# Experts in units of 32 tokens on four column quarters of the array, and weights in transfers of 4 KB rows

## The reference

```python
idx, wts = route(hf, w_router, b_router)       # best group of 4, then the top 2 of its 4 experts
# the rows of each expert are gathered, then
(silu(xe @ w_gate[e]) * (xe @ w_up[e])) @ w_down[e]   # D=1024 -> F=512 -> D=1024
# and each token adds its two rows, weighted by wts
```

## Time and profile before

| | us |
|---|---|
| median of 3 runs (2388.24 to 2390.66) | 2388.29 |
| profiled execution | 2393.53 |
| its span | 2391.9 |

### The profile page before, as it was taken

The page is one execution under the profiler, slowest core; times in us unless marked ns, Lnnn a source line. Parts: engine busy times, 40 slices in busy tenths (PEclk is TensorE's granted clock), DMA queues, the critical chain, the costliest instruction groups (busy, mean ns, idle before and its releaser), DMA issues.

```text
span 2391.9 us, 33087 instructions
## 1 busy us (share of the span) xinstructions
PE 2167.1 (91%) x12218; PEld 1202.3 (50%) x12219; DVE 1155.4 (48%) x2059; ACT 743.6 (31%) x1571; POOL 273.3 (11%) x465
## 2 busy tenths in 40 slices
PE   6999999999999399999998599989984899999991
PEld 2444444456666355555554367655443455555551
DVE  2355500678997622222222699999845122222225
ACT  3111100567775222222222411026252222222222
POOL 0000010000000112111112300000000111112113
PEclk8999999899999699999999699999986999999996
DMA  9166410003301665566666400300025777624646
GB/s 390 72 246 246 176 54 0 36 19 150 150 10 52 266 247 187 222 256 254 254 254 254 158 36 35 140 36 1 0 97 202 310 322 286 261 86 154 246 153 224
DMA packets 51578, 391.49 MB, mean 164 GB/s; under 512 B 9009, under 2 KB 9265, under 8 KB 33841
## 3 DMA queue, kind: packets, MB, share of 16 engines
q1 hardware_dynamic: 22514, 298.12, 30.9%
q0 software_dynamic: 28992, 92.40, 11.4%
HBM read 340.12 MB, written 50.37 MB: 163 GB/s over the span
## 4 chain that ended last, share of the span: by engine, by line
PE 77%; DVE 13%; DMA 5%; issue 2%; ACT 2%; POOL 0%; POOLq 0%; SPq 0%; DVEq 0%
PE ps L1417 21%; PE ps L1399 12%; PE ps L1265 9%; DVE kv L1134 8%; PE ps L1513 5%; PE ps L1283 5%; PE ps L1339 4%; PE ps L1297 3%; PE ps L1310 3%; PE ps L1322 3%; PE ps L1481 3%; DMA expert_rows<-hT 3%; PE ps L1406 2%; PE ps L1386 1%; DMA hT<-h_rows,idx_now 1%
## 5 line engine op out<-in xcount | busy, mean ns | idle before, releaser
L1134 DVE SCALAR_TENSOR_TENSOR kv<-kv,cols 128x640 f32<-128x640 f32 (+1 forms) x390 | 305.1, 782 | 13.3
L1417 PE MATMUL ps<-kv,hT 128*64 128x256 f32 x2624 | 290.9, 379 | 0.9 <-DMA kv<-in_w_gate_up 0.9
L1417 PE MATMUL ps<-ring,hT 128*64 128x256 f32 x2496 | 281.0, 384 | 10.8 <-issue 5.1
L644 ACT ACTIVATE hT<-ps 128x128 f32<-128x128 f32 x160 | 44.4, 277 | 679.8 <-PE ps L1417 679.8
L1417 PEld LDWEIGHTS ps<-kv,hT 128*64 128x64 f32 x2624 | 201.3, 137 | 101.4 <-issue 26.4
L1417 PEld LDWEIGHTS ps<-ring,hT 128*64 128x64 f32 x2496 | 193.2, 139 | 110.4 <-issue 39.7
L1453 PE MATMUL ps<-hT,ring 128*128 128x320 f32 (+1 forms) x768 | 225.4, 455 | 6.3 <-ACT hT L525 6.3
L1265 PE MATMUL ps<-hT,ring 128*128 128x512 f32 x512 | 226.5, 601 | 1.6 <-ACT hT L525 1.6
L904 DVE TENSOR_TENSOR_SCAN pbuf<-hT 128x128 f32<-128x128 f32 (+7 forms) x128 | 173.3, 1354 | 47.6 <-ACT hT L576 47.3
L1453 PEld LDWEIGHTS ps<-hT,ring 128*128 128x128 f32 x768 | 147.2, 193 | 81.1 <-ACT hT L525 7.0
L1069 DVE COPY hT<-ps 128x128 f32<-128x128 f32 x160 | 46.7, 292 | 267.3 <-PE ps L1406 267.3
(11 more groups left out here) (240 smaller groups left out, 2475.5 us busy)
## 6 DMA issues: line engine op xcount, KB each, us to landing
ring<-in_w_gate_up SPq DMA_DIRECT2D x32, 2048.0 KB, 12.5
kv<-in_w_gate_up SPq DMA_DIRECT2D x32, 2048.0 KB, 13.1
kv<-in_w_ada SPq DMA_DIRECT2D x20, 2048.0 KB, 7.6
ring<-in_w_down SPq DMA_DIRECT2D x16, 2048.0 KB, 13.9
kv<-in_w_down SPq DMA_DIRECT2D x16, 2048.0 KB
expert_rows<-hT POOLq DMA_DIRECT2D x160, 128.0 KB, 2.5
expert_rows<-ring POOLq DMA_DIRECT2D x2, 8192.0 KB, 24.7
ring<-in_w_in SPq DMA_DIRECT2D x8, 2048.0 KB, 8.1
```

What stands on the lines that cost most here:

```text
L1134: ins = V.scalar_tensor_tensor(new, old, w_dw_c[:, c, k:k + 1], new, ALU.mult, ALU.add)
L1417: ins = mm(bank(f)[UNIT * t:UNIT * t + UNIT, 0:2 * P], xT[:, c, :], wset[s][t][:, 512 * c + 256 * f:512 * c + 256 * f + 256], start=(c == ...
```

## The change

Units of 32 tokens; each expert gets at least `MINBLK = 2` blocks. A row is split over four partition quarters of 256 features, and matmuls have 32 stationary columns on one quarter of the array's columns. In gate/up a quarter makes gate and up of 128 hidden features, all four in one bank; down has 4 chunks x 4 quarters of 256 columns. One silu, one product and one transpose per block replace two of each.

Around it: down of block b-1 now stands behind gate/up of block b. Each expert's first block is written apart from the loop, since its down pass belongs to the expert before. Two gather buffers `xg[0]`, `xg[1]`; GpSimd copies a gathered block to `xs`, from which TensorE transposes. `yo_all` has two slots, and ScalarE stores them, in four transfers of 32 rows x 1 KB. Each weight piece goes in four transfers with rows of 4 KB. `TABLE` grows from 50 to 96. Semaphores of the weights are shared by the layers, and a small activation ahead of the final gathers (`rows_stored`) loads the table for the square root.

```diff
-UNIT = 64
-MAXBLK = (2 * T + E * (UNIT - 1)) // UNIT + 1
-TABLE = MAXBLK + 2
+UNIT = 32
+QUARTERS = P // UNIT
+MINBLK = 2
+MAXBLK = 2 * T // UNIT + MINBLK * (E - 2)
+TABLE = MAXBLK + 4
+PARTS = 4
+QUARTER = D // QUARTERS
...
+        xg = [hflat[:, QUARTER * u:QUARTER * (u + 1)] for u in range(2)]
+        xs = hflat[:, 768:768 + QUARTER]
+        xT = hflat[:, 512:768].rearrange("p (c t) -> p c t", c=DC)
+        sg, ha, haT = hflat[:, 1024:1152], hflat[:, 1152:1280], hflat[:, 1280:1408]
+        yo_all = hflat[:, 1792:1792 + 2 * QUARTER]
...
-                sp.dma_start(wset[s][k], src).then_inc(w_loaded[l][s][k], 16)
+                for q in range(PARTS):
+                    sp.dma_start(part(wset[s][k], q), part(src, q)).then_inc(w_loaded[s][k], 16)
...
-                        sp.wait_ge(up_done[l], 2 * ends)
+                        sp.wait_ge(up_done[l], ends)
...
+                            src = w_gate_up[ds(4 * i + 2 * s + 2 * l * E + k, 1)].rearrange("a p n -> (a p) n")
+                            for q in range(PARTS):
+                                sp.dma_start(part(wset[s][k], q), part(src, q)).then_inc(w_loaded[s][k], 16)
...
+                        src = w_down[ds(2 * i + s + l * E, 1)].rearrange("a p n -> (a p) n")
+                        for q in range(PARTS):
+                            sp.dma_start(part(wset[s][2], q), part(src, q)).then_inc(w_loaded[s][2], 16)
...
+                def gather(u):
...
+                        out=xg[u], out_offset=None, in_=h_dram[l].rearrange("t (q d) -> (t q) d", q=QUARTERS),
+                        in_offset=bass.IndirectOffsetOnAxis(ap=idx_now[:, u:u + 1], axis=0)).then_inc(x_gathered[l][u], 16)
...
+                pairs = pool.value_load(bounds[0:1, E + 1:E + 2], min_val=1, max_val=(MAXBLK + 1) // 2)
+                pool.wait_ge(x_gathered[l][0], 16)
+                nc.gpsimd.tensor_copy(xs, xg[0]).then_inc(idx_made[l], 1)
+                nc.gpsimd.tensor_copy(idx_now[:, 0:1], slot_tok[:, 2:3]).then_inc(idx_made[l], 1)
+                pool.wait_ge(idx_made[l], 5)
                 gather(0)
...
+                with pool.Fori(0, pairs) as i:
+                    for u in (1, 0):
+                        n = 2 * i + 2 - u
+                        pool.wait_ge(x_gathered[l][u], 16 * i + 32 - 16 * u)
+                        pool.wait_ge(x_turned2[l], n)
+                        nc.gpsimd.tensor_copy(idx_now[:, u:u + 1], slot_tok[:, ds(n + 2, 1)])
+                        nc.gpsimd.tensor_copy(xs, xg[u]).then_inc(x_ready[l], 1)
+                        pool.wait_ge(table_made[l], 1)
+                        pool.wait_ge(x_ready[l], n)
+                        gather(u)
+                pool.wait_ge(rows_stored[l], 1)
...
+                def silu(b):
+                    act.wait_ge(up_done[l], b + 1)
+                    nc.scalar.activation(sg, bank(0)[:, 0:P], ACT.Silu).then_inc(silu_done[l], 1)
+                def store(b, half):
+                    act.wait_ge(y_kept[l], b + 2)
+                    for q in range(QUARTERS):
+                        act.dma_start(y_dram[l][ds(b * UNIT, UNIT), QUARTER * q:QUARTER * (q + 1)],
+                                      yo_all[UNIT * q:UNIT * (q + 1), ds(half * QUARTER, QUARTER)]
+                                      ).then_inc(y_stored[l], 16)
...
+                blocks = act.value_load(bounds[0:1, E:E + 1], min_val=MINBLK * E, max_val=MAXBLK)
+                silu(0)
+                keep(1)
+                silu(1)
+                keep(2)
+                store(0, 0)
+                with act.Fori(0, blocks - 2) as b:
+                    silu(b + 2)
+                    keep(b + 3)
+                    act.wait_ge(y_stored[l], 16 * QUARTERS * b + 16 * QUARTERS)
+                    store(b + 1, (b + 1) & 1)
+                pairs = act.value_load(bounds[0:1, E + 1:E + 2], min_val=1, max_val=(MAXBLK + 1) // 2)
+                act.wait_ge(x_gathered[l][0], 16 * pairs + 32)
+                act.wait_ge(x_gathered[l][1], 16 * pairs + 16)
+                store(blocks - 1, (blocks + 1) & 1)
+                act.wait_ge(y_stored[l], 16 * QUARTERS * blocks)
+                nc.scalar.activation(table_ahead[:, l:l + 1], eps[:, :], ACT.Sqrt).then_inc(rows_stored[l], 1)
...
+                def gated_half(b):
+                    dve.wait_ge(silu_done[l], b + 1)
+                    V.tensor_tensor(ha, sg, bank(0)[:, P:2 * P], ALU.mult).then_inc(ha_made[l], 1)
+                def keep_ha(b):
+                    dve.wait_ge(ha_turned[l], b + 1)
+                    V.tensor_copy(haT, bank(2)[:, 0:P]).then_inc(haT_kept[l], 1)
+                def keep_y(b, half):
+                    dve.wait_ge(down_done[l], b + 1)
+                    V.tensor_tensor(yo_all[:, ds(half * QUARTER, QUARTER)], bank(6)[:, 0:QUARTER],
+                                    bcC[:, 0:QUARTER], ALU.mult).then_inc(y_kept[l], 1)
...
+                dve.wait_ge(gate_loaded, 80 * (l + 1))
+                blocks = dve.value_load(bounds[0:1, E:E + 1], min_val=MINBLK * E, max_val=MAXBLK)
+                gated_half(0)
+                keep(1)
+                keep_ha(0)
+                for b in (1, 2):
+                    gated_half(b)
+                    keep(b + 1)
+                    keep_y(b - 1, (b + 1) % 2)
+                    keep_ha(b)
+                dve.wait_ge(y_stored[l], 16 * QUARTERS)
+                with dve.Fori(0, blocks - 3) as b:
+                    gated_half(b + 3)
+                    keep(b + 4)
+                    keep_y(b + 2, b & 1)
+                    keep_ha(b + 3)
+                    dve.wait_ge(y_stored[l], 16 * QUARTERS * b + 32 * QUARTERS)
+                keep_y(blocks - 1, (blocks + 1) & 1)
...
+                def turn_rows():
+                    for j in range(2):
+                        nc.tensor.transpose(bank(4 + j)[:, 0:P], xs[:, P * j:P * (j + 1)], ident[:, :]
+                                            ).then_inc((x_turned, x_turned2)[j][l], 1)
+                def gate_up(b, s):
+                    pe.wait_ge(xT_kept[l], b + 1)
+                    pe.wait_ge(xT_kept2[l], b + 1)
+                    for c in range(DC):
+                        for q in range(QUARTERS):
+                            ins = mm(bank(0)[UNIT * q:UNIT * (q + 1), 0:2 * P], xT[:, c, :],
+                                     wset[s][q // 2][:, 512 * c + 256 * (q % 2):512 * c + 256 * (q % 2) + 256],
+                                     start=(c == 0), stop=(c == DC - 1), skip_group_check=True)
+                    ins.then_inc(up_done[l], 1)
+                def turn_ha(b):
+                    pe.wait_ge(ha_made[l], b + 1)
+                    nc.tensor.transpose(bank(2)[:, 0:P], ha, ident[:, :]).then_inc(ha_turned[l], 1)
+                def down(b, s):
+                    pe.wait_ge(haT_kept[l], b + 1)
+                    pe.wait_ge(y_kept[l], b + 1)
+                    for f in range(QUARTERS):
+                        for q in range(QUARTERS):
+                            ins = mm(bank(6)[UNIT * q:UNIT * (q + 1), 0:QUARTER], haT[:, UNIT * f:UNIT * (f + 1)],
+                                     wset[s][2][:, D * f + QUARTER * q:D * f + QUARTER * (q + 1)],
+                                     start=(f == 0), stop=(f == QUARTERS - 1), skip_group_check=True)
+                    ins.then_inc(down_done[l], 1)
+                def expert(i, s, very_first=False):
+                    first = pe.value_load(bounds[0:1, ds(2 * i + s, 1)], min_val=0, max_val=MAXBLK)
+                    end = pe.value_load(bounds[0:1, ds(2 * i + s + 1, 1)], min_val=MINBLK, max_val=MAXBLK)
+                    for k in range(2):
+                        pe.wait_ge(w_loaded[s][k], 16 * PARTS * (E // 2 * l + 1) + 16 * PARTS * i)
+                    if very_first:
+                        gate_up(0, s)
+                        pe.wait_ge(x_ready[l], 1)
+                        turn_rows()
+                        turn_ha(0)
+                    else:
+                        gate_up(first, s)
+                        pe.wait_ge(x_ready[l], first + 1)
+                        turn_rows()
+                        down(first - 1, 1 - s)
+                        turn_ha(first)
+                    with pe.Fori(first + 1, end) as b:
+                        gate_up(b, s)
+                        pe.wait_ge(x_ready[l], b + 1)
+                        turn_rows()
+                        pe.wait_ge(w_loaded[s][2], 16 * PARTS * (E // 2 * l + 1) + 16 * PARTS * i)
+                        down(b - 1, s)
+                        turn_ha(b)
...
+                pe.wait_ge(idx_made[l], 4)
+                turn_rows()
+                expert(0, 0, very_first=True)
+                expert(0, 1)
+                with pe.Fori(1, E // 2) as i:
...
+                        expert(i, s)
+                last = pe.value_load(bounds[0:1, E:E + 1], min_val=MINBLK * E, max_val=MAXBLK)
+                down(last - 1, 1)
```

(22 more changed lines are left out.)

170 lines of the change are left out of this document (43 added, 127 removed).

## The result

The changed kernel takes **2395.60 us** (median of 11 runs, 2389.21 to 2396.86) where the kernel before takes 2388.29 (11 runs beside them, 2386.37 to 2391.17). The ratio is 1.0023, with a 95% interval of 1.0014 to 1.0033. The forecast was 2352, and faster.

A forecast was written before the change was run, and what follows sets the result against it. TensorE was taken as the bound, blocks times its block time. Loops fall from 958.2 to 915.7 us, a gain of 42.5 less 6.6 outside, 35.9, so 2388.3 becomes 2352; range 2330 to 2402.

The forecast's parts named there:

- Number of blocks, time of a block: Expert loops: 144 blocks of 6.04 us on TensorE, 869.8 us against 933.6 before.
- Silu, product, copies hidden, no table load: ScalarE and VectorE work inside a block hides behind TensorE with 0.4 us of cover; table load stands ahead of the loop.
- Stores on ScalarE: Four store issues per block behind the product: 2.2 us (1.4 to 4.4), ending about 0.9 us before the next silu.
- net gain forecast: Whole kernel: 42.5 us gained in the expert loops, less 6.6 outside them, 35.9 us.
- Changes of expert: TensorE's sequencer late at each new expert: 0.65 us eight times, 1.25 seven times, 14.0 a layer, 28 in all.
- The rest of the sum: Remaining terms: loop ends 5.6 us, cold matmuls 4.3, late weights 4, meeting issues 4, outside the loops 6.6.
- waits at a stage's end: Ends of the expert loops: last down pass no longer beside another block, 2.8 us a stage, 5.6 in all.
- Outside the loops: Larger slot table, small steps and an extra copy on the path: 3.3 us a layer, 6.6 in all.
- ScalarE becomes the bound (slower): Rival, stores in ScalarE's order: issues at 0.9 us each cost 58 us, giving 2410; chance 0.12.
- the sign set down: ScalarE in the profile after: silu released by something other than TensorE (ScalarE's issues) would show the forecast wrong.
- Weights late in the second layer: Start of the second layer, four two-block experts: weights land late, 4 us of waiting, between 0 and 10.
- 4 KB rows: Weight transfers: same bytes, four times the transfers, twelve issues of 0.54 per expert, about 10% off the rate for rows.

The follow-up runs named there:

- e7: Changed kernel with each weight transfer inside the expert loop cut to a quarter of its bytes, same number of issues (output not the reference's): 2353.39 us, ratio 0.9860.
- e8: Changed kernel with ScalarE storing one quarter of a block's columns in one transfer, not four (output not the reference's): 2345.23 us, ratio 0.9818.
- e1: Changed kernel with two stores of results in flight, even and odd blocks counted on separate semaphores: 2356.80 us, ratio 0.9868.
- e5: Changed kernel with two stores in flight, and each w_in and w_out piece after a layer's experts in four transfers: 2354.54 us, ratio 0.9867.
- e6: e5 with TensorE's read of an expert's end moved behind its first gate/up, and every second expert's start not read again: 2342.26 us, ratio 0.9813.

## Why the prediction was wrong

- **Number of blocks, time of a block:** right. 144 blocks, and a median of 6.08 us a block in e7 and e8, 6.04 predicted. Four column quarters ran at the rate read off the router's logits; the 2.38 of 3 by the Trainium skill ("TensorE: Matmul & The Clock Gate", Part 3) does not agree with the 3.66 us of gate/up.
- **Silu, product, copies hidden, no table load:** right; the silu starts 0.1 us or less behind gate/up wherever no store holds it.
- **Stores on ScalarE, the step that failed.** "Four cost 1.4 to 4.4 us; I take 2.2": 1.9, right. "They end at about 8.8, 0.9 before the silu" supposed that they start when the product is there. They start after the last landing, for which I took the median of 2.5 and left the 11.3 to a rival. But landings are of two kinds, 2.7 us from the first issue without weights and 6.5 in the median with them, and the DMA engines are busy for over half of a stage (share 0.65 and 0.60). The median of the kernel before hid the second kind, which 66 of its 160 stores already were. Priced: 959.4 - 922.0 = 37.4 us between the changed kernel and e1, which is all of the net gain forecast (35.9).
- **Changes of expert:** 28 us predicted, too high. In e5 a change took 0.32 and 0.9 us over a block, not 0.65 and 1.25: some 17 us in all. e6 against e5 took out 12.9 of profiled loop time (918.7, which is 451.5 and 467.2, to 905.8).
- **The rest of the sum:** e1's stages are 922.0 where 915.7 was forecast, and its 2356.8 is within 5 us of the 2352. Outside the loops the change added 1.5 us (2394.6 - 959.4 against 2391.9 - 958.2), not 6.6. That e1 comes so near is in part luck: the terms for changes of expert and outside the loops were too high by some 11 and 5 us, and the blocks (0.04 us each, 5.8 in all), late weights and waits at a stage's end took more than theirs.
- **Rivals:** "ScalarE becomes the bound (slower)" had the place, and named the wait in half a sentence; it put the price on the issues and a chance of 0.12 on it. Its 2410 was 14 too high. The silu released by something other than TensorE was the sign set down, and it is what the profile shows.
- **Weights late in the second layer:** 4 us predicted, between 0 and 10. In e6, where little else waits, TensorE's waits in the second stage (us, times, longest) make 7.8, within the range:

```profile
PE ps L1487 <- DMA ring<-in_w_gate_up: 5.2, 3, 2.7
PE ps L1487 <- DMA kv<-in_w_gate_up: 2.6, 1, 2.6
```

- **4 KB rows:** I priced them for the weights alone. Their worth lay in the stores.

## What to carry to other kernels

A wait for a transfer inside an engine's order costs its whole round, issue and landing, against the period of the loop; take the landing from the stretch where the DMA engines are full, not the median of the run. When blocks are halved, each such round must fit in half the time: give it a second semaphore and a second buffer before moving it. Short rows in a big stream let small transfers through; and a store put into one issue can land later than in four; look at its outermost dimension, since a spread over fewer engines is the likely reason here, though not a tested one.

## Not expected of the hardware

- The same 128 KB of a block under weights: last packet 7.2 us after the first issue in four transfers over 4 KB weight rows, 11.6 over 16 KB rows, 11.0 in one transfer over 4 KB rows; without weights 2.7, 2.7 and 3.0.
- Two reads of a number by TensorE's sequencer (0.30 us each) ahead of an expert's first gate/up were part of a gap of 0.83 us; one read behind those matmuls, while they still ran, left no gap at the same place.
- Beside streaming weights a store's first packet mostly went out 3.4 to 4.2 us after its issue, not 0.84; with rows of 16 KB it was no later (3.7 us, against 4.2 with 4 KB, at the two stores compared). What holds it stays open.
